# Expert layer of a hybrid encoder block: the last 32 tokens' u products taken from fetched rows instead of the dense product

## What is computed

```
scores = einsum("thcd,hcnd->thcn", qry, sub_keys)
s_top, i_top = top_k(scores, 16)                  # two half-keys per head
best_s, best_pos = top_k(all pair sums, 16)       # 16 experts per head
expert_idx = take_along_axis(pair indices, best_pos)
gates = softmax(best_s)
act = gelu(einsum("td,thkd->thk", h, expert_u[expert_idx]))
out = einsum("thk,thkd->td", act * gates, expert_v[expert_idx])
```

## Time and profile before

| | |
|---|---|
| median of 3 runs (lowest, highest) | 1995.24 us (1991.93, 1995.54) |
| span of the profiled execution | 1990.5 us, 4.7 us less than that median |
| PE busy | 1935.9 us, 97% |
| DVE busy | 1497.9 us, 75% |
| ACT busy | 723.5 us, 36% |
| moved by DMA | 465.94 MB, mean 234 GB/s |
| indirect row fetches | 128, 134.23 MB |

### The profile page before, as it was taken

How to read it: one execution, slowest core, us unless ns; L and a number is a source line. 1 busy time by engine, 2 the same in 40 slices (tenths; PEclk the granted TensorE clock), 3 DMA queues, 4 the chain that set the end, 5 groups by cost and what they waited for, 6 DMA issues and landing times.

```text
span 1990.5 us, 27945 instructions
## 1 busy us (share of the span) xinstructions
PE 1935.9 (97%) x10357; PEld 1710.3 (86%) x10357; DVE 1497.9 (75%) x2735; ACT 723.5 (36%) x1331; POOL 420.1 (21%) x231
## 2 busy tenths in 40 slices
PE   7999999999999999999999999999999999999998
PEld 4789777889877988999999999999988888888887
DVE  4776645364576537788889999996688898889986
ACT  4110233010351343343443444444444444444443
POOL 0333211444102023001111511111221222222210
PEclk9999999999999999999999999999999999999999
DMA  7235311353112432257668688888999999999993
GB/s 276 86 115 195 121 56 40 130 200 117 63 43 85 149 106 85 95 171 273 226 217 276 221 319 303 300 304 299 397 387 401 401 400 401 399 401 395 402 378 131
DMA packets 212644, 465.94 MB, mean 234 GB/s; under 512 B 15625, under 2 KB 157121, under 8 KB 193345
## 3 DMA queue, kind: packets, MB, share of 16 engines
q1 hardware_dynamic: 193408, 330.43, 47.7%
q0 software_dynamic: 18432, 134.23, 17.1%
q10 hardware_dynamic: 704, 0.04, 0.0%
HBM read 410.12 MB, written 54.53 MB: 233 GB/s over the span
## 4 chain that ended last, share of the span: by engine, by line
PE 43%; DMA 9%; DVE 4%; ACT 1%; issue 1%; SPq 1%; DVEq 0%; POOLq 0%; POOL 0%; ACTq 0%
PE xin_ps_u L2148 22%; PE xin_out L2192 16%; DMA experts_hot<-act_scratch 6%; PE xin_out L2170 4%; DMA con_raw<-in_expert_u 2%; DMA con_raw<-in_expert_v 1%; DVE over_v_vlo L2453 1%; DVE in_ulo L2304 1%; DVE experts_acc L1960 1%; SPq L2120 1%; DVE experts_rows L1941 1%; DVE xin_wt L2450 0%; ACT in_uhi L2221 0%; DVE xin_wlo L2455 0%; ACT L2263 0%
## 5 line engine op out<-in xcount | busy, mean ns | idle before, releaser
L1934 POOL DMA_INDIRECT experts_rows<-in_expert_rows,experts_idx x128 | 204.7, 1599 | 915.7 <-DVE experts_acc L1960 779.3
L2148 PE MATMUL xin_ps_u<-con_h_hi,in_uhi 128*128 128x384 f32 x1024 | 349.0, 341 | 11.3 <-DVE in_ulo L2304 9.1
L2148 PE MATMUL xin_ps_u<-con_h_hi,in_ulo 128*128 128x384 f32 x1024 | 343.3, 335 | 0.0
L2148 PE MATMUL xin_ps_u<-con_h_lo,in_uhi 128*128 128x384 f32 x1024 | 343.2, 335 | 0.0
L2192 PE MATMUL xin_out<-over_v_vhi,xin_whi 128*128 128x512 f32 x768 | 238.7, 389 | 2.3 <-DVE xin_wlo L2455 2.2
L2192 PE MATMUL xin_out<-over_v_vhi,xin_wlo 128*128 128x512 f32 x768 | 238.5, 389 | 0.0
L2192 PE MATMUL xin_out<-over_v_vlo,xin_whi 128*128 128x512 f32 x768 | 238.4, 389 | 0.0
L2304 DVE TENSOR_TENSOR in_ulo<-con_raw,in_uhi 128x1024 fp32r<-128x1024 f32 x127 | 155.2, 1222 | 81.2 <-ACT in_uhi L2221 78.7
L2148 PEld LDWEIGHTS xin_ps_u<-con_h_hi,in_uhi 128*128 128x128 f32 x1024 | 193.2, 189 | 15.6 <-DVE in_ulo L2304 13.0
L2148 PEld LDWEIGHTS xin_ps_u<-con_h_lo,in_uhi 128*128 128x128 f32 x1024 | 193.3, 189 | 0.0
L2148 PEld LDWEIGHTS xin_ps_u<-con_h_hi,in_ulo 128*128 128x128 f32 x1024 | 192.9, 188 | 0.0
(11 more groups left out here) (445 smaller groups left out, 3738.5 us busy)
## 6 DMA issues: line engine op xcount, KB each, us to landing
con_raw<-in_expert_u SPq DMA_DIRECT2D x128, 512.0 KB, 4.7
con_raw<-in_expert_v SPq DMA_DIRECT2D x128, 512.0 KB, 11.9
con_raw<-in_w_in SPq DMA_DIRECT2D x36, 1024.0 KB, 6.2
act_scratch<-in_act SPq DMA_DIRECT2D x128, 192.0 KB, 2.2
experts_hot<-act_scratch SPq DMA_DIRECT2D x128, 192.0 KB, 12.1
...
```

Of the source, the lines that this page charges most:

```text
L1934: pool.indirect_dma_start(out=self.rows[:, r % ROWS, :], out_offset=None, in_=table, in_offset=at).then_inc(self.row_in[r % ROWS], 16)
L2148: mm = pe.matmul(ps_u[s % 2][:, 0:TD], a[s % 2][:, k, :], m[:, k, P:T], start=(i == 0), stop=(i == 3 * KD - 1))
```

## The change

The last 32 tokens (of tile 3) leave the dense u product. `TU` is 352, and u matmuls, gelu and `act_scratch` rows are 352 wide. The v pass stays 384 wide.

- For these 32 tokens the 128 chosen u rows are fetched by POOL as half rows (4 KB). Partitions are filled with 4 groups of the 32 tokens, each group with another 32 of the 128 slots, so 32 fetches of 128 half rows do it: 16 "side" entries of two fetches in one row buffer. DVE makes two dots per side entry against `con.h3`, the tokens' h in four copies; there is no `weigh` and no `add`.
- The 32x32 dots per group go through one gelu on ACT, through four small DMAs on SP into one row per token, and are multiplied with the gates on DVE. PE turns the product, and it takes the gates' place in the one-hot products of the last four hot steps. What these then write to `gate_scratch` for the 32 tokens is the finished coefficient, so in the v pass the multiplication with activations covers 352 columns only.
- Routing runs over the tiles in the order 0, 3, 1, 2, as tile 3's indices are needed early. The side entries lie in steps 40 to 74 (every fourth step to 52, then 56 to 59, then every second step to 74).
- These places were held by entries of tile 0. All 128 of those remain: 40 are now in the u pass and 88 in the v pass. In the tail every step has an entry (20, not 15).
- `finish_block` ends with 8 transposes and two ACT copies that make `con.h3`; `query_block` makes its copies with three DMAs.
- The v pass multiplies in place in the tile of gates, in two instructions (320 and 32 columns). A new wait on `wlo_done` stands before each load of that tile. The PE loop over three groups of hot steps is written out. Several tiles are placed elsewhere to make room.

```diff
+SIDE = 32
+SIDE_GROUPS, TU = P // SIDE, TD - SIDE
+ORDER = (0, 3, 1, 2)
...
+SIDE_FROM, SIDE_WAIT = N_SEARCH + 2 * R_STEPS + 8, N_HOT0 + N_HOT - SIDE // G_TOK - 3
 def slots_of_steps():
...
-        if (n < N_ROUTE and n % 4 == 0) or N_ROUTE <= n < N_HOT0 or (N_HOT0 <= n < N_HOT0 + N_HOT and n % 2 == 0) or (n >= N_HOT0 + N_HOT and n % 4 != 3):
+        if (n < N_ROUTE and n % 4 == 0) or N_ROUTE <= n < N_HOT0 or (N_HOT0 <= n < N_HOT0 + N_HOT and n % 2 == 0) or n >= N_HOT0 + N_HOT:
+            if n >= SIDE_FROM and len(side) < SIDE // 2:
+                side.append(e)
...
+        if e in SIDE_OF:
+            for half, c in enumerate(SIDE_OF[e]):
+                pool.indirect_dma_start(out=self.rows[:, s, half * D:(half + 1) * D], out_offset=None, in_=halves,
+                                        in_offset=bass.IndirectOffsetOnAxis(ap=self.side_at[:, c:c + 1], axis=0)
+                                        ).then_inc(self.row_in[s], 16)
...
-                        mm = pe.matmul(ps_u[s % 2][:, 0:TD], a[s % 2][:, k, :], m[:, k, P:T], start=(i == 0),
+                        mm = pe.matmul(ps_u[s % 2][:, 0:TU], a[s % 2][:, k, :], m[:, k, P:P + TU], start=(i == 0),
...
+                if n == SIDE_FROM - 4:
+                    side_indices()
+                if n == SIDE_WAIT:
+                    side_activations()
...
+                    sp.wait_ge(wlo_done, n - 3)
                     sp.dma_start(g4[k % 2], gmat[k].rearrange("b j x -> j b x")).then_inc(g_in[k % 2], 16)
...
+                if n == SIDE_WAIT - 2:
+                    last = SIDE_ENTRIES[-1]
+                    act.wait_ge(got.row_free[last % ROWS], last // ROWS + 1)
+                    act.activation(got.side_dots[:], got.side_dots[:], ACT.Gelu).then_inc(got.side_raw_done, 1)
...
+                if e == SIDE_ENTRIES[0]:
+                    pool.wait_ge(got.side_at_in, 16 * SIDE_GROUPS)
...
+            def side_coefficients():
+                dve.wait_ge(got.side_act_in, 16 * SIDE_GROUPS)
+                some = slice(P - SIDE, P)
+                dve.tensor_tensor(got.side_gate[some, :], got.side_gate[some, :], got.side_act[some, :],
+                                  ALU.mult).then_inc(got.side_coef_done, 1)
+            def side_slots():
+                dve.wait_ge(late_t, 1)
+                dve.tensor_copy(slot[2][:, TU:TD], out[0][0][:, P - SIDE:P]).then_inc(late_done, 1)
...
-                wait(dve, wlo_done, n - 1)
-                dve.tensor_tensor(blocks(wt[n % 2][:]), blocks(a[s]), g4[n // RING % 2][:, :, s * 64:(s + 1) * 64],
-                                  ALU.mult).then_inc(wt_done, 1)
+                w = weights(n)
+                for some, src in WEIGHTED:
+                    op = dve.tensor_tensor(w[:, some[0], some[1]], w[:, some[0], some[1]],
+                                           a[s][:, src].rearrange("p (b t) -> p b t", b=some[0].stop - some[0].start), ALU.mult)
+                op.then_inc(wt_done, 1)
```

More of the change, by code:

```diff
@@ L1475, in _, with turn_back_last @@
                 unit(i)
+            def turn_back_last():
+                pe.wait_ge(modded, KD * NT)
+                for half in range(2):
+                    pe.wait_ge(freed[2 + half], U // 4)
+                    for j in range(4):
+                        mm = pe.transpose(bank[2 + half][:, j * P:(j + 1) * P], h[1][:, 4 * half + j, :], con.ident[:])
+                    mm.then_inc(back, 1)
             def first_queries(c, ks, some):
@@ L1560, in _ @@
             modulate(3)
+            act.wait_ge(ss2_done, NT)
+            for half in range(2):
+                act.wait_ge(back, 3 + half)
+                act.activation(con.h3[:, half * 512:(half + 1) * 512], bank[2 + half][:], ACT.Copy).then_inc(h3_kept, 1)
         @block.vector
@@ L1924, in __init__ @@
         self.idx = al.sb("idx", [P, SLOTS], U32)
-        self.gate, self.dots, self.raw, self.coef = [al.sb(n, [P, SLOTS]) for n in ("gate0", "dots", "raw", "coef")]
-        self.row_in = [al.sem(f"row_in{i}") for i in range(ROWS)]
-        self.idx_done, self.dot_done, self.raw_done, self.coef_done, self.acc_done = map(
-            al.sem, ("idx_done", "dot_done", "raw_done", "coef_done", "acc_done"))
-    def fetch(self, pool, r, table):
-        at = bass.IndirectOffsetOnAxis(ap=self.idx[:, r:r + 1], axis=0)
-        wait(pool, self.acc_done, r - ROWS + 1)
-        pool.indirect_dma_start(out=self.rows[:, r % ROWS, :], out_offset=None, in_=table,
-                                in_offset=at).then_inc(self.row_in[r % ROWS], 16)
@@ L1937, in dot @@
-    def dot(self, dve, r, h0):
-        u = self.rows[:, r % ROWS, 0:D]
-        dve.wait_ge(self.row_in[r % ROWS], 16 * (r // ROWS + 1))
-        dve.scalar_tensor_tensor(out=u, in0=u, scalar=1.0, in1=h0, op0=ALU.mult, op1=ALU.mult,
-                                 accum_out=self.dots[:, r:r + 1]).then_inc(self.dot_done, 1)
-    def weigh(self, act, r):
+        self.gate, self.coef, self.side_gate = [al.sb(n, [P, SLOTS]) for n in ("gate0", "coef", "side_gate")]
+        self.side_at, self.side_dots, self.side_act = al.sb("side_at", [P, SIDE], U32), al.sb("side_dots", [P, SIDE]), side_act
@@ new lines, in fetch @@
+    def fetch(self, pool, e, rows, halves):
+        s = e % ROWS
+        wait(pool, self.row_free[s], e // ROWS)
+        if e in SIDE_OF:
[3 more added lines that the diff above has]
+                                        ).then_inc(self.row_in[s], 16)
+        else:
+            r = MAIN_OF[e]
+            pool.indirect_dma_start(out=self.rows[:, s, :], out_offset=None, in_=rows,
+                                    in_offset=bass.IndirectOffsetOnAxis(ap=self.idx[:, r:r + 1], axis=0)
+                                    ).then_inc(self.row_in[s], 16)
@@ new lines, in dot @@
+    def dot(self, dve, e, con):
+        s = e % ROWS
+        dve.wait_ge(self.row_in[s], 16 * sum(2 if x in SIDE_OF else 1 for x in range(s, e + 1, ROWS)))
+        if e in SIDE_OF:
+            for half, c in enumerate(SIDE_OF[e]):
+                u = self.rows[:, s, half * D:(half + 1) * D]
+                op = dve.scalar_tensor_tensor(out=u, in0=u, scalar=1.0, in1=con.h3[:], op0=ALU.mult, op1=ALU.mult,
+                                              accum_out=self.side_dots[:, c:c + 1])
+                op.then_inc(self.row_free[s] if half else self.side_dot_done, 1)
+        else:
+            r, u = MAIN_OF[e], self.rows[:, s, 0:D]
+            dve.scalar_tensor_tensor(out=u, in0=u, scalar=1.0, in1=con.h0[:], op0=ALU.mult, op1=ALU.mult,
+                                     accum_out=self.coef[:, r:r + 1]).then_inc(self.dot_done, 1)
@@ L2025, in experts_block @@
         shifted = [part([PH, TOPK], U32) for i in range(3)]
+        side_idx = part([1, SLOTS], U32).rearrange("p a b -> p (a b)")
         rank, key, gate = [[part([PH, TOPK]) for c in range(2)] for n in range(3)]
-        gate0 = got.gate[:].rearrange("p (h k) -> p h k", h=PH)
+        gate0, gate3 = [x[:].rearrange("p (h k) -> p h k", h=PH) for x in (got.gate, got.side_gate)]
+        gate_of = lambda q: {0: gate0, ORDER.index(NT - 1): gate3}.get(q, gate[q % 2])
         flat = lambda ap: ap.rearrange("p h k -> p (h k)")
@@ L2179, in _ @@
             pe.wait_ge(slots_done, ND)
-            for gi in pairs(pe, N_HOT // G_STEPS, True):
+            for gi in range(N_HOT // G_STEPS):
                 for q in range(G_STEPS):
+                    if G_STEPS * gi + q == N_HOT - SIDE // G_TOK - 1:
+                        turn_side()
                     every(N_HOT0 + G_STEPS * gi + q, q)
```

154 lines of the change are left out of this document (104 added, 50 removed).

## The result

The changed kernel takes 2002.85 us (median of 7 runs, 1998.89 to 2005.20), the kernel before took 1994.91 beside it (7 runs, 1990.92 to 1997.64). The ratio is 1.0041, with a 95% interval of 1.0029 to 1.0053: slower by 0.4%, about 8 us. The profiled execution has a span of 2001.3 us against 1990.5, which is 10.8 longer. The forecast was 2006, slower, 10.8 on the span.

The account below looks back on a forecast made before the run. PE was taken to set the pace, with DMA at its ceiling in tail and v pass. Terms -13 - 8 + 1.8 + 12 + 23 - 5 = +10.8 us gave median 2006; own range 1998 to 2017, over all 1980 to 2018.

Parts of the forecast that it names:

- u products 0.160 apart: u matmuls at 352 columns start 0.160 us apart, so a u step falls from 4.16 to 3.84 us.
- The rival that they do not get faster: Weight loads bound the u matmul stream, so 352 columns change nothing: +32 us, median 2027, chance 0.02.
- Steps 0 to 59, -13: First 60 u steps, with routing: narrower products save 13 us, between 5 and 16.
- Hot stage, -8: Hot stage: a step falls from 5.94 to 5.72 us over about 37 steps, saving 8 us, between 6 and 12.
- The bound of 5.72: Hot stage: the bound passes from PE at 5.94 us a step to DVE's five large operations at 5.72.
- Small additions, +1.8: Block end, copies of h and short DVE operations cost 1.8 us together; the new waits cost nothing.
- Tail, +12: Tail: five more entries, 4.9 MB at 395 GB/s, cost 12 us as the stage waits for DMA.
- v pass, +23 less 5 of slack: v pass: 11 more entries cost 23 us of DMA; stretches under 400 GB/s give back 5, between 0 and 8.
- Nothing hides an entry: Tail and v pass: DVE runs in order, so a late row holds its next operation and PE waits.
- DMA has room: Rival: DMA can take more, v pass costs 0 and tail +2; sum -17 us, median 1978, chance 0.23.
- Half and half: Rival: 20 of the 35 us arrive and routing gives 16; sum -2 us, median 1993 to 1999, chance 0.12.
- DVE on top: Rival: v pass in-place products bring DVE to 4.35 us a step, adding 13 us; median 2019, chance 0.10.

Follow-up runs that it names:

- e2: Changed kernel without side entries, all tile 0 entries in their old places, u products of the last 32 tokens left out: 1966.46 us, ratio 0.9861.
- e7: Changed kernel with the eight entries of steps 0 to 59 moved to steps where routing puts little on DVE: 1996.72 us, ratio 1.0017.
- e1: Kernel before with only the 16 entries moved, nothing narrower and nothing fetched for the last 32 tokens: 2024.39 us, ratio 1.0152.
- e3: Changed kernel, but 11 of the 88 v pass entries fetch 512 bytes a row, DVE's work unchanged: 1984.55 us, ratio 0.9951.
- e4: Changed kernel, but DVE's dot and add cover 64 of 1024 columns for 11 v pass entries, rows fetched whole: 2002.34 us, ratio 1.0043.
- e5: Changed kernel with the gated one-hot tile made by eight small DVE instructions in place of two large ones: 1998.85 us, ratio 1.0024.
- e6: As e5, with 12 more entries in the hot stage and so 76 in the v pass: 2000.57 us, ratio 1.0031.
- e9: As e6 with e7's places; in the hot stage ACT scales rows and POOL, not DVE, makes 28 adds: 2035.81 us, ratio 1.0211.
- e11: As e9, without the fused one-hot tile: 2037.65 us, ratio 1.0217.

## Why the prediction was right

Its direction, its range and its reason held. Term by term:

- **u products 0.160 apart:** exact. The rival that they do not get faster is gone.
- **Steps 0 to 59, -13:** measured -10.4. The gain without side work is 12.9 (e2, 248.6 against 261.6), so the narrower products give what was forecast, and the side entries cost 2.6, all of it in steps 40 to 59. The prediction has no term for them here: "pairs of steps hold ten operations as before" was worked out for the hot stage only. In routing, the two dots of a side entry fall on steps that are already heavy for DVE (5.63 to 5.88 us at 41, 45, 49 and 53). With the same number of entries at other steps e7 is 4.5 us faster, 1.7 of it before step 40, where only tile 0's entries were moved.
- **Hot stage, -8:** measured -11.7. The bound of 5.72 held: 37 steps at 5.695 for 5.947 give 9. The other 2 us are the last step, where DVE had waited 3.5 us before and does not now.
- **Small additions, +1.8:** the block starts 3.4 us later, which the runs can't put down to them. Steps 102 and 104 are 0.7 us longer together, by the short DVE operations. None of the new waits at steps 99 to 104 shows in a chain.
- **Tail, +12:** measured +6.2. **v pass, +23 less 5 of slack:** measured +22.7. Together 30 against 28.9. The mis-sized term is the tail's, and with it the slack of 5 that was taken off behind it. The tail moved more bytes a second than the 395 that the sum used (406 over 96 us, or 11 x 96 = 1.1 MB, 2.6 us), and what it left late came on top in the v pass, so that the slack of 5 did not appear. That second half is argued, no run isolates it, and the other 3 us of the tail stay open. For it speaks that PE is idle for 6.1 of the first 53 us of the v pass (1447 to 1500), where it was idle for 0.3 of 40 before. Of the two gaps that the slack was read from, the one at the end did fill up in part (383 GB/s from 1900 to 1960, for 355). e1, with full-width products, has the same tail as after (+6.2); in e3, e4, e5 and e7, which share after's tail, it is 4.7 to 9.0 longer than before, so the term is known to some 2 us.
- **Nothing hides an entry:** right, as e1 to e4 show. PE's idle time in the v pass is 16.4 us, within the 15 to 20 foretold. The v pass is 22.7 longer, more than the 15 to 20 given among the signs, though just what the term of 23 says; idle time grew by 15.0 of these 22.7 us, and the lower clock behind two stalls is some 3 more, estimated as twice the 1.6 above.

The rivals: *DMA has room* (0.23) falls with e3 against e4. Before, the highest slice was 402 GB/s; after, the v pass ran at 398 where 420 were asked for. The tail's slice reached 414, in e1 415. The Trainium skill, DMA: Bandwidth & Descriptors, section Where 436 GB/s comes from, has a ceiling of 435 GB/s; no slice of these kernels comes to it, and the v pass with its mix of 8 KB rows and short pieces stays at about 400. *Half and half* wanted 20 of the 35 us to arrive and 28.9 did; its time, 1993 to 1999, is 4 to 10 us short, though the tail showed its mechanism. *DVE on top* falls with e1 and e4.

The sum of 10.8 on the span came out to the tenth, which is luck: terms were off by 3 to 6 us both ways, and the medians differ by 7.9. Two things in the prediction's account of its numbers don't follow from its terms: their ends, added up, give 1995 to 2026 and not 1998 to 2017, and two rivals' times (1978 and 2027) lie outside the range over all.

No version that computes everything beats the kernel before. e2 gives what the narrow products would be worth if the side work and 16 entries had a free place, 28 us. e6 shows that the hot stage has no such place on DVE, e9 to e11 that handing adds to POOL makes none, e1 and e3 that tail and v pass have none on DMA.
